# An encoder layer in fp32: the output projection changed from eight tile products to four pairs of seven block products

## The reference

```
n  = rmsnorm(x, g_mix);  z = n @ w_in
a_out = (y @ w_glu_a) * sigmoid(y @ w_glu_b)        # y: gelu of the state-space branch, width 512
merged = sigmoid(gate_ssm) * a_out + sigmoid(gate_pool) * p_out
h  = x + merged @ w_out                             # the output projection, 1024 x 1024
n2 = rmsnorm(h, g_ffn)
h  = h + (silu(n2 @ w_ffn_gate) * (n2 @ w_ffn_up)) @ w_ffn_down
y  = rmsnorm(h, g_final)
```

## Time and profile before

| | |
|---|---|
| median of three runs | 1279.55 us |
| profiled execution, its time | 1278.96 us |
| its span | 1277.1 us |
| PE busy | 1243.8 us (97%) |
| DVE, POOL, ACT busy | 697.0, 550.4, 408.9 us |

### The profile page before, as it was taken

The page is one execution under the profiler, slowest core; times in us unless marked ns, Lnnn a source line. Parts: engine busy times, 40 slices in busy tenths (PEclk is TensorE's granted clock), DMA queues, the critical chain, the costliest instruction groups (busy, mean ns, idle before and its releaser), DMA issues.

```text
span 1277.1 us, 20140 instructions
## 1 busy us (share of the span) xinstructions
PE 1243.8 (97%) x8670; PEld 1233.1 (97%) x8670; DVE 697.0 (55%) x835; ACT 408.9 (32%) x585; POOL 550.4 (43%) x335
## 2 busy tenths in 40 slices
PE   7999999999999999998899999999999999999997
PEld 7999899999999999998899999999999999999997
DVE  6795598828556632269944343434343434343545
ACT  4613311425222223224342424242424242424421
POOL 2312122211212244424984747474747474747731
PEclk9999999999999999999999999999999999999998
DMA  9269522154254431112112121212121212121203
GB/s 323 88 147 173 118 75 89 34 127 154 72 181 148 161 124 36 50 34 66 34 37 63 37 64 35 65 36 65 35 65 36 65 35 66 35 66 34 66 25 112
DMA packets 126290, 104.71 MB, mean 82 GB/s; under 512 B 9568, under 2 KB 112096, under 8 KB 126208
## 3 DMA queue, kind: packets, MB, share of 16 engines
q1 hardware_dynamic: 125056, 103.46, 28.0%
q10 hardware_dynamic: 1152, 0.06, 0.1%
HBM read 82.80 MB, written 17.43 MB: 78 GB/s over the span
## 4 chain that ended last, share of the span: by engine, by line
PE 86%; DVE 8%; issue 2%; ACT 1%; DMA 1%; POOL 1%; SPq 0%; DVEq 0%; ACTq 0%; POOLq 0%
PE psum L565 32%; PE psum L768 30%; PE psum L804 14%; PE psum L840 4%; DVE S L1395 1%; PE psum L755 1%; PE psum L585 1%; DVE sc_a L1395 1%; DVE low_a L1395 1%; DVE low_b L1395 1%; DMA xs<-in_x_turned 1%; DVE sc_b L1395 1%; PE psum L659 1%; POOL w_lo L1293 1%; PE psum L675 1%
## 5 line engine op out<-in xcount | busy, mean ns | idle before, releaser
L1293 POOL TENSOR_TENSOR w_lo<-stage,w_hi 128x1024 fp32r<-128x1024 f32 (+1 forms) x50 | 121.4, 2428 | 424.2 <-ACT w_hi L902 411.8
L768 PE MATMUL psum<-op_hi,w_hi 128*128 128x264 f32 x1120 | 228.3, 285 | 4.4 <-issue 1.6
L768 PE MATMUL psum<-op_hi,w_lo 128*128 128x264 f32 x1120 | 226.5, 283 | 0.0
L1395 DVE TENSOR_TENSOR hT<-psum,hT 128x1056 f32<-128x1056 f32 (+2 forms) x104 | 113.0, 1087 | 150.1 <-PE psum L804 80.8
L768 PEld LDWEIGHTS psum<-op_hi,w_hi 128*128 128x128 f32 x1120 | 173.3, 189 | 4.9 <-issue 3.4
L768 PEld LDWEIGHTS psum<-op_hi,w_lo 128*128 128x128 f32 x1120 | 173.9, 189 | 0.0
L565 PE MATMUL psum<-x_hi,w_hi 128*128 128x352 f32 x720 | 155.0, 324 | 1.1 <-DVE UP L1395 0.5
L565 PE MATMUL psum<-x_hi,w_lo 128*128 128x352 f32 x720 | 154.2, 323 | 0.0
L565 PE MATMUL psum<-x_lo,w_hi 128*128 128x352 f32 x720 | 154.2, 323 | 0.0
L768 PE MATMUL psum<-low_a,w_hi 128*128 128x264 f32 x720 | 146.3, 285 | 0.0
L565 PEld LDWEIGHTS psum<-x_hi,w_hi 128*128 128x128 f32 x720 | 121.5, 188 | 2.2 <-issue 1.2
(11 more groups left out here) (264 smaller groups left out, 2261.1 us busy)
## 6 DMA issues: line engine op xcount, KB each, us to landing
stage<-in_w_in SPq DMA_DIRECT2D x22, 512.0 KB, 4.7
stage<-in_w_ffn_up SPq DMA_DIRECT2D x14, 512.0 KB, 3.8
stage<-in_w_ffn_down SPq DMA_DIRECT2D x12, 512.0 KB, 3.9
pair_y<-in_w_ffn_gate SPq DMA_DIRECT2D x12, 512.0 KB, 4.6
stage<-in_w_ffn_gate SPq DMA_DIRECT2D x10, 512.0 KB, 4.2
pair_y<-in_w_ffn_down SPq DMA_DIRECT2D x10, 512.0 KB, 4.4
xs<-in_x_turned SPq DMA_DIRECT2D x8, 528.0 KB, 8.3
mp_scratch<-gate_t SPq DMA_DIRECT2D x8, 528.0 KB, 3.4
```

Of the source, the lines that this page charges most:

```text
L768: mm = pe.matmul(out[:, b, :], w[:, slot, k * P:(k + 1) * P], x[:, b * HB:(b + 1) * HB], start=(first and k == 0 and step == 0), stop=(k = ...
L1293: pool.tensor_tensor(to[:, slot, 0:cols], stage[:, slot, 0:cols], hi[:, slot, 0:cols], ALU.subtract).then_inc(lo_ready, 1)
L1395: return dve.tensor_tensor(out, a, b, op)
```

## The change

The output projection is made as the FFN's pairs are: four pairs of output tiles, each with seven block products of 24 matmuls of 264 columns (`out_product`, `out_pair`), in the order B11, T1, T2, B21, T3, B22, T4. The operand blocks are the halves of `merged` and their sums: with the first half of the channels (tiles 0 to 3) B11 and B12, with the second half B21 and B22, T1 = B12 - B11, T2 = B22 - T1, T4 = B21 - T2, T3 = B22 - B12. DVE makes them in `merge`, tile by tile as the gated unit delivers: for n < 4 the two halves and T1; for n >= 4 the two halves and T2, T4, T3; ACT writes their high parts, DVE their low parts. The weights of a pair land in `stage` (both slots), POOL makes four sums of blocks and seven low parts, ACT seven high parts; `w_hi` and `w_lo` are used as four slots of 512 columns. The squares are now summed by DVE (`add_squares`), no longer by POOL.

```diff
+            def out_product(p, i, q):
+                j, slot, out = ORDER[i], (7 * p + i) % 4, couple(q)
+                pe.wait_ge(out_lo, 7 * p + i + 1)
+                for k in range(KH):
+                    if p == 0:
+                        pe.wait_ge(m_lo_ready, m_count(j, k))
+                    for step, (w, x) in enumerate(((w_hi4, m_high), (w_hi4, m_low), (w_lo4, m_high))):
+                        for b in range(2):
+                            mm = pe.matmul(out[:, b, :], w[:, slot, k * P:(k + 1) * P], x(j, k)[:, b * HB:(b + 1) * HB],
...
+                mm.then_inc(out_done, 1)
+            def out_pair(p, banks):
+                qa, qb, qc = banks
+                if p >= 2:
+                    pe.wait_ge(out_taken, 7 * (p - 1))
+                out_product(p, 0, qb)
+                if p:
+                    pe.wait_ge(out_taken, 7 * p - 3)
+                else:
+                    pe.wait_ge(evac_done, T_GLU + 15)
+                out_product(p, 1, qc)
+                pe.wait_ge(out_taken, 7 * p + 1)
+                out_product(p, 2, qb)
...
+            pe.wait_ge(out_taken, 7 * OUT_PAIRS - 1)
             pe.wait_ge(lo_ready, S_FFN + 1)
             tile(T_FFN, bank_a, 0, ALL, hg_hi, hg_lo, ready=hg_lo_ready, between=sum_squares)
```

```diff
@@ SP
+            sp.wait_ge(y_lo_ready, KS)
...
+            def load_out(p):
+                if p:
+                    sp.wait_ge(out_lo, 7 * p)
+                else:
+                    sp.wait_ge(lo_ready, S_GLU + KD)
+                for m in range(2):
+                    sp.dma_start(pair_x[:, m, :].rearrange("p (k n) -> p k n", n=P),
+                                 w_o[:, :, (2 * p + m) * P:(2 * p + m + 1) * P]).then_inc(out_in, 16)
...
+            load_out(0)
+            sp.wait_ge(tile_done, T_OUT)
+            for k in range(KD // 2):
+                load_residual(k)
+            load_out(1)
+            for k in range(KD // 2, KD):
+                load_residual(k)
+            load_out(2)
+            load_out(3)
+            sp.wait_ge(out_lo, 7 * OUT_PAIRS)
@@ ACT
+            def out_high(p, i):
+                c = 7 * p + i
...
+                if c < 4:
+                    act.wait_ge(tile_done, T_GLU + (14 if c < 2 else 16))
+                else:
+                    act.wait_ge(out_done, c - 3)
+                act.activation(w_hi4[:, c % 4, :], out_raw(i), ACT.Copy).then_inc(out_hi, 1)
@@ DVE, after merge(0) to merge(7)
+            def out_add(p, i, q, bank):
+                dve.wait_ge(out_done, 7 * p + i + 1)
...
+                tt_(b2(out_quarter(p, q)), couple(bank), b2(out_quarter(p, q)), ADD).then_inc(out_taken, 1)
...
+            for p in range(OUT_PAIRS):
+                qa, qb, qc = (0, 2, 1) if p % 2 else (1, 3, 0)
+                dve.wait_ge(xt_in[2 * p], 16)
+                out_add(p, 0, C11, qb)
+                if p:
+                    dve.wait_ge(out_taken, 7 * p)
+                    low_tile(2 * p - 2)
...
```

More of the change, by code:

```diff
@@ L695, in _ @@
             pe.wait_ge(y_lo_ready, KS)
-            with pe.Fori(0, 4) as m:
+            for m in range(4):
                 for r in range(2):
@@ L725, in spread_rows @@
                     mm.then_inc(row_ready, 1)
[L728 to L736, removed]
+            def out_product(p, i, q):
[7 more added lines that the diff above has]
+                            mm = pe.matmul(out[:, b, :], w[:, slot, k * P:(k + 1) * P], x(j, k)[:, b * HB:(b + 1) * HB],
+                                           start=(i in (0, 1, 3) and k == 0 and step == 0), stop=(k == KH - 1 and step == 2),
+                                           skip_group_check=True)
+                mm.then_inc(out_done, 1)
@@ L896, in _, with split @@
         def _(act):
-            def split(s, slot, landed, done, cols=SLAB, to=w_hi):
+            def split(s, slot, landed, done, cols=SLAB, to=w_hi, freed=None):
                 act.wait_ge(stage_in[slot], landed)
+                if freed is not None:
+                    act.wait_ge(out_done, freed)
                 if done is not None:
@@ L1051, in glu @@
                 act.activation(b3(glu_b[:, :]), B3, ACT.Sigmoid).then_inc(b_sig, 1)
-                split(n + (S_GLU + 2), r, count, None)
-                act.wait_ge(merged_ready, n + 1)
-                act.activation(at_tile(x_hi, n), at_tile(merged, n), ACT.Copy).then_inc(m_hi_ready, 1)
+                if n < KD - 2:
+                    split(n + (S_GLU + 2), r, count, None)
+                else:
+                    for i in (0, 1) if n == KD - 2 else (2, 3):
+                        out_high(0, i)
+                act.wait_ge(merged_ready, n + 1)
+                k, base = n % KH, KH + 3 * (n - KH)
+                if n < KH:
+                    high_piece(B11, k)
+                    high_piece(T1, k, n + 1)
+                else:
+                    high_piece(B21, k)
+                    high_piece(T2, k, base + 1)
+                    high_piece(T4, k, base + 2)
+                    high_piece(T3, k, base + 3)
+                    high_piece(B22, k)
             for g in range(4):
@@ L1808, in _, with add_squares @@
                                          SUB).then_inc(hg_lo_ready, 1)
+            def add_squares(n):
+                if n == 0:
+                    return
+                dve.wait_ge(sq_ready, n + 1)
+                if n >= 2:
+                    dve.wait_ge(sq_used, n - 1)
+                tt_(out_sq[:, :], out_sq[:, :], rstd_row[:, :], ADD).then_inc(sq_used, 1)
+            for p in range(OUT_PAIRS):
+                qa, qb, qc = (0, 2, 1) if p % 2 else (1, 3, 0)
+                dve.wait_ge(xt_in[2 * p], 16)
+                out_add(p, 0, C11, qb)
+                if p:
+                    dve.wait_ge(out_taken, 7 * p)
+                    low_tile(2 * p - 2)
+                dve.wait_ge(xt_in[2 * p + 1], 16)
+                out_add(p, 1, C22, qc)
+                if p:
+                    add_squares(2 * p - 2)
+                out_add(p, 2, C12, qb)
+                if p:
+                    low_tile(2 * p - 1)
+                out_add(p, 3, C11, qa)
+                if p:
+                    add_squares(2 * p - 1)
+                out_add(p, 4, C22, qb)
+                out_add(p, 5, C12, qc)
+                out_add(p, 6, C21, qb)
+            dve.wait_ge(out_taken, 7 * OUT_PAIRS)
+            for n in (KD - 2, KD - 1):
+                low_tile(n)
+                add_squares(n)
             dve.wait_ge(ss_turned, 1)
```

191 lines of the change are left out of this document (143 added, 48 removed).

## The result

| | before | after |
|---|---|---|
| median of 4 runs (lowest to highest), us | 1279.11 (1277.32 to 1282.06) | 1291.04 (1290.26 to 1294.48) |
| ratio, 95% interval | | 1.0093 (1.008 to 1.0106) |
| profiled execution, us; its span; mean granted clock | 1278.96; 1277.1; 0.994 | 1290.95; 1289.1; 0.986 |
| gated unit, first product to first product of the projection | 92.29 | 93.54 |
| output projection, to the FFN's first product | 92.16 | 102.16 |

A forecast was written before the change was run, and what follows sets the result against it. PE was taken as the bound, busy for 97% of the span. On the profiled 1278.96 us, -10.4 + 1.3 + 12.1 + 7.7 + 1.5 = +12.2 gave 1291.2, stated as 1291.5; range for 8 in 10: 1280 to 1299.

The forecast's parts named there:

- PE's saving: Output projection: 28 block products of 2.92 us, 81.8 us against 92.16, so -10.4 us.
- DVE in tiles 4 to 6: Gated unit: DVE's ten half operations and POOL make PE wait once for a PSUM bank, +1.3 us (0 to 2.6).
- The first pair: Projection's start: PE waits 1.7 us before the second product and 10.4 before the third, for the first residual addition; +12.1 us.
- The weight cycle: Later pairs and first FFN tile: reloading `stage` after the seventh low part takes longer than PE's pair; +7.7 us (0 to 15).
- The clock: Behind the wait of about 10 us PE runs at the lower clock for a while; +1.5 us (1.3 to 2.9).
- Edits at nothing: SP's wait for `y_lo_ready`, residual tile loads, DVE's additions of squares, the spreading and written-out loops: taken to cost nothing.
- Rival A: First pair costs only its floor of 4.4 us and the weight cycle fits: about 1279, no change; chance 0.13.
- Rival B: All is hidden: residual additions slip in and PE runs through, 1269 to 1275 us; chance 0.06.

The follow-up runs named there:

- x1_early: Changed kernel with the first pair's first residual addition moved on DVE before the last gated tile's product with the sigmoid: 1286.22 us, ratio 1.0063 to the kernel before.
- x3: Changed kernel with the second pair's weights landing in the sigmoids' dead memory, loaded during the first pair: 1288.28 us, ratio 1.0068 to the kernel before.
- x7: Changed kernel with the first FFN slab landing in the feed-forward tile's memory instead of `stage`: 1288.19 us, ratio 1.0058 to the kernel before.
- x4: Changed kernel with DVE adding only 16 columns of the squares for tiles 1 to 5, false 1/rms, for timing only: 1287.46 us, ratio 1.0063 to before.
- x2: Changed kernel with 60 useless matmuls filling PE's wait for the first residual addition: 1287.91 us, ratio 1.0071 to the kernel before.
- x10: x8 with T2's low part made before T3's sum and the second residual addition on the last gated tile: 1276.81 us, ratio 0.9974 to the kernel before.
- x8: Changed kernel with the edits of x9, x3 and x7 together: 1277.98 us, ratio 0.9989 to the kernel before.
- x9: Changed kernel with the first pair's first three residual additions moved early among DVE's work on tile 7: 1286.78 us, ratio 1.0053 to the kernel before.
- x6: x5 with the first FFN slab landing in the memory of the last tile of hg: 1282.97 us, ratio 1.0022 to the kernel before.
- x5: Changed kernel with x1_early's and x3's edits and, in tiles 4 to 7, T2's and B21's low parts before T3's sum: 1287.97 us, ratio 1.0059 to before.

## Why the prediction was right

It said 1291.5 and 1291.04 was measured. By its steps:

- **PE's saving, -10.4: right.** 28 products of 2.92 us are 81.8; the projection took 102.16, and the waits and the clock below (9.9 + 7.2 + 3.3) explain the difference.
- **DVE in tiles 4 to 6, +1.3: right.** One wait of 1.02 for `glu_a`, the gated unit 1.25 longer. The estimate's own figures, 13.0 less 11.5, give 1.5.
- **The first pair, +12.1: right in mechanism, 2.2 too large.** Measured 1.2 before the second product and 8.7 before the third, 9.9 in all. The mis-sized term is the price of DVE's operations in tile 7's round. The estimate had 2.4 for the product with the sigmoid, 7.0 for ten halves and 3.6 for POOL beside them, 13.0 in all from E + 4.6. Measured from the rows above: 2.3, then 8.6 from 444.67 to 453.27, of which the two holds by POOL (2.29 for two halves, 1.77 for one) are 2.1 and the ten halves 6.5, 10.9 in all from E + 4.1 (E is 438.24). Halves that follow one another start every 0.62 to 0.65 us, and POOL met DVE three times, not four. The addition began at E + 15.0 and not at E + 17.6. x1_early shows the cause: with the addition in front the third product started with no wait (its last k-term then waited 2.1 for T2's low part).
- **The weight cycle, +7.7: right.** Intervals of 22.8, 24.7 and 24.5 us against 22.3, 24.5 and 24.5. By the starts of the products, the waits for `w_lo` are 5.0 (2.5 around the third pair's start, 2.5 at the fourth's) and the slab's is 2.2, which makes 7.2. x3 and x7 show the transfer's part, x4 DVE's.
- **The clock, +1.5: too small.** Behind the long wait it cost 1.8 (three terms of six matmuls from 454.01 to 458.04, 4.03 us against 2.19). The estimate left out the second stretch, behind the 2.36 us wait at the fourth pair: another 1.4 (4.35 us for a product of 2.92). It had also read its own row short: 6.07 us less 2.9 is 3.2, not 2.9. The notion that a part of the clock's price is absorbed by a later wait for weights did not hold: x2, without the first slow stretch, had a projection 2.7 us shorter and shorter waits for `w_lo`.
- **Edits at nothing: right.** Head of the FFN 19.76 against 19.87, spreading wait 1.39 as before.

1.25 + 9.9 + 7.2 + 3.3 - 10.4 = 11.25, as measured (93.54 + 102.16 less 92.29 + 92.16). Two terms were 2.2 and 0.5 too large and the clock 1.8 too small, so most of the error cancelled. Another part is luck of the execution: the sum is 11.25 and the medians differ by 11.9, and the forecast itself rounds 1291.16 + 0.6 down to 1291.5. The total is nearer than the parts deserve. Rival A's floor of 4.4 for the first pair held for the additions behind the ten halves; a rearrangement goes below it: x10 has waits of 1.05 + 1.45 + 0.5 there. Rival B's fall came from the operations ahead of the first addition, as said.

The Trainium skill, in "SBUF — State Buffer", section "SBUF: two separate sides", has VectorE (DVE) with two SBUF inputs and GpSimd (POOL) exclude each other for a whole instruction. The rows agree for both directions: VectorE's 1.26 became 2.28, GpSimd's 1.3 became 2.17, and VectorE's read of PSUM with an SBUF operand stayed at 1.25 beside GpSimd's 1.59 (why that one took 1.59 and not 1.3, nothing here shows).

## What to carry to other kernels

When products become fewer, count the operand work that each first product waits for on the other engines, and put the operations that free PSUM ahead of those that make later operands: one addition moved by a few places was worth 5.5 us of PE's waiting. A buffer that is reloaded once per round only makes a cycle; price load, conversions and the next load as one loop, and follow it to the first consumer behind the loop. Go on after the first link: the early additions alone left the kernel 0.5% slower than before, and only with the two moved landings was the loss gone.

## What the runs showed of the hardware

The lower clock behind short waits is not decided by the wait's length alone. A wait of 2.74 us inside the third product of x8 was followed by a granted clock of 1.00, and one of 2.76 at the same product of x9 by 0.61 (four matmuls in 0.75 and in 1.25). Windows of x8, then of x9:

```profile
450.00:454.00 4.00, 3.95 (x32) 3.95 (x33) 4.00 (x5) 1.53 (x3) 3.49 (x2) 1.00 1.03 405
```

```profile
450.00:454.00 4.00, 3.74 (x20) 3.74 (x21) 4.00 (x6) 1.73 (x4) 3.28 (x2) 0.61 0.00 0
```

PE had done the same before both. The DMA traffic differs (405 GB/s against 0), but it is no answer: x1's 2.13 us at the same product was followed by 1.00 with no traffic at all, and x6's 2.37 us by 0.62 with 126 GB/s. Of seventeen waits between 1.95 and 3.0 us in the stretches read here, thirteen were followed by a slow stretch and four were not (after's 2.05, x1's 2.13, x5's 2.35, x8's 2.74); of those from 1.0 to 1.9 us none was. Outside the stretch even that is no rule: all twelve profiles show a wait of 1.69 us at 133 to 134 us, in a part of the program that none of the edits touches, and in x7's alone a slow stretch follows:

```profile
134.00:138.00 4.00, 3.96 (x42) 3.80 (x42) 0.00 (x0) 2.01 (x6) 0.00 (x0) 0.57 0.00 0
```

So the same code gets a slow stretch in one execution and none in another. What decides stays open. A slow stretch cost 1.4 to 1.8 us beyond the wait, and more where it lasted: 2.5 us behind the long wait of x4 (5.40 for a product of 2.92), and the FFN's head of x3 is 2.8 us longer.
